# A hybrid decoder layer on one core: z of each pair projected one pair later, and the mixed rows loaded in twos into the low part and split in place

## The reference

```python
h = rms_norm(x, norm_g)
proj = jnp.einsum('bsd,de->bse', h, w_in)
(aq, ak, av, az, bq, bk, bv, bz, bf, cq, ck, cv, cz, cr) = jnp.split(proj, SPLIT_IDX, axis=-1)
out_a = dilated_mixture(rms_norm(aq) * scale, rms_norm(ak), av)        # 12 heads of 64, three dilated windows
out_b = forgetting_attention(rms_norm(bq) * scale, rms_norm(bk), bv, log_f)   # 8 heads of 64
out_c = rms_norm(gla_chunked(cq, ck, cv, log_a), gla_out_gain)         # 4 heads of 192
mixed = concatenate([out_a * silu(az), out_b * silu(bz), out_c * silu(cz)])   # widths 768, 512, 768
return x + einsum('bse,ed->bsd', mixed, w_out)
```

## Time and profile before

| what | value |
|---|---|
| median of 3 runs | 2240.43 us (2240.12 to 2241.71) |
| profiled execution, its own time | 2238.91 us |
| its span | 2237.2 us |
| mean granted clock of TensorE | 0.984 |
| busy: PE, DVE, ACT, POOL | 2155.4, 987.0, 865.1, 238.8 us |
| moved by DMA | 203.23 MB, mean 91 GB/s |

### The profile page before, as it was taken

One profiled execution on the slowest core, in us unless ns is written; L12 is line 12 of the kernel. 1 busy time (PEld: TensorE's weight loads), 2 busy tenths in 40 slices (PEclk: granted clock), 3 DMA queues, 4 the chain that ended last, 5 costly groups with the idle time before them and its releaser, 6 DMA issues.

```text
span 2237.2 us, 30415 instructions
## 1 busy us (share of the span) xinstructions
PE 2155.4 (96%) x11016; PEld 1822.3 (81%) x11016; DVE 987.0 (44%) x1639; ACT 865.1 (39%) x1466; POOL 238.8 (11%) x141
## 2 busy tenths in 40 slices
PE   6999999999989999999999999999999968999999
PEld 5788888888878888888888888888888857778887
DVE  6611346354444544445454545445454555522122
ACT  7311234434354444444444445444444444311110
POOL 0000143331411000101000000001010000000000
PEclk9999999999999999999999999999999979999999
DMA  6322324233322222212222222313222254332234
GB/s 215 82 67 75 94 71 110 62 91 100 84 89 67 71 85 67 85 52 80 70 71 70 66 81 81 95 56 94 70 93 65 67 178 151 118 122 91 80 124 144
DMA packets 190458, 203.23 MB, mean 91 GB/s; under 512 B 16168, under 2 KB 139096, under 8 KB 189232
## 3 DMA queue, kind: packets, MB, share of 16 engines
q1 hardware_dynamic: 173664, 171.80, 26.4%
q10 hardware_dynamic: 16720, 30.45, 3.6%
HBM read 152.38 MB, written 49.83 MB: 90 GB/s over the span
## 4 chain that ended last, share of the span: by engine, by line
PE 85%; DVE 4%; issue 3%; ACT 3%; DMA 3%; POOL 1%; ACTq 0%; DVEq 0%; SPq 0%; POOLq 0%
PE acc L1619 18%; PE acc L1621 17%; PE acc L1620 17%; PE turned L1813 3%; PE pv L1826 3%; PE pv L1825 3%; PE scores L1802 2%; PE scores L1799 2%; DMA w_raw<-in_w_out_dram 2%; PE pv L1707 1%; PE acc L1905 1%; PE acc L1907 1%; PE acc L1906 1%; PE scores L1906 1%; PE scores L1905 1%
## 5 line engine op out<-in xcount | busy, mean ns | idle before, releaser
L1619 PE MATMUL acc<-act_hi,w_hi 128*128 128x512 f32 x1856 | 741.7, 400 | 7.0 <-DVE w_lo L1172 2.5
L1621 PE MATMUL acc<-act_hi,w_lo 128*128 128x512 f32 x1856 | 727.4, 392 | 0.0
L1620 PE MATMUL acc<-act_lo,w_hi 128*128 128x512 f32 x1856 | 726.6, 391 | 0.0
L1172 DVE TENSOR_TENSOR w_lo<-w_raw,w_hi 128x512 fp32r<-128x512 f32 x224 | 181.5, 811 | 581.3 <-ACT w_hi L779 581.0
L1619 PEld LDWEIGHTS acc<-act_hi,w_hi 128*128 128x128 f32 x1856 | 351.1, 189 | 78.3 <-DVE w_lo L1172 5.1
L1621 PEld LDWEIGHTS acc<-act_hi,w_lo 128*128 128x128 f32 x1856 | 350.3, 189 | 76.4
L1620 PEld LDWEIGHTS acc<-act_lo,w_hi 128*128 128x128 f32 x1856 | 351.5, 189 | 67.1
L779 ACT ACTIVATE w_hi<-w_raw 128x512 fp32r<-128x512 f32 x224 | 140.6, 628 | 302.7 <-PE acc L1621 256.4
L1056 ACT ACTIVATE prob<-prob,neg_max 128x128 f32<-128x128 f32 (+7 forms) x160 | 124.4, 777 | 293.3 <-DVE neg_max L1445 293.3
L1461 DVE TENSOR_TENSOR pt_lo<-turned,pt_hi 128x128 fp32r<-128x128 f32 (+7 forms) x160 | 120.9, 755 | 160.1 <-ACT pt_hi L1064 159.3
L1826 PE MATMUL pv<-pt_lo,v_st 128*128 128x128 f32 x720 | 170.5, 276 | 0.0
(11 more groups left out here) (266 smaller groups left out, 2807.9 us busy)
## 6 DMA issues: line engine op xcount, KB each, us to landing
w_raw<-in_w_in_dram SPq DMA_DIRECT2D x240, 256.0 KB, 2.9
proj_scratch<-stage ACTq DMA_DIRECT2D x116, 256.0 KB, 2.1
w_raw<-in_w_out_dram SPq DMA_DIRECT2D x94, 256.0 KB, 3.1
raw<-proj_scratch SPq DMA_DIRECT2D x20, 512.0 KB, 3.4
raw<-mixed_scratch SPq DMA_DIRECT2D x16, 512.0 KB, 4.3
res<-in_x_dram SPq DMA_DIRECT2D x24, 256.0 KB, 5.8
out_dram<-res SPq DMA_DIRECT2D x24, 256.0 KB, 3.0
sq<-proj_scratch SPq DMA_DIRECT2D x10, 512.0 KB, 3.5
```

The lines of the kernel that those rows point to most:

```text
L1172: dve.tensor_tensor(w_lo[:, slot, :], w_raw[:, slot, :], w_hi[:, slot, :].bitcast(F32), ALU.subtract)\
L1619: pe.matmul(acc, hi, xh, start=first, stop=False)
L1620: pe.matmul(acc, hi, xl, start=False, stop=False)
L1621: mm = pe.matmul(acc, lo, xh, start=False, stop=end)
```

## The change

- Counts: `C_FIRST` is gone, the plain stage has one group less. The heads' spare groups are shifted: z of GLA is projected inside the heads, v of pair 0 alone in the group ahead of the pairs (`S_FIRST_V`).
- Body p projects q, k, v of pair p+1 and z of pair p (`columns_of`). z of pair p is loaded into `vz` in body p+1 and bounded, put through the gate and multiplied there; the outputs of pair p wait in the new tile `o_full` (1024 wide) and meet the gate in one product at slot 8 of body p+1 (`gated`).
- The last pair gets the group `S_LAST_Z` in its slots 0 to 7. The early quarters start at slot 8 and end at slot 32, evenly. z of pair 9 is loaded, bounded and put through in slots 15 to 18, in the tile `last_gate`.
- Mixed rows are loaded in twos (1 MB) into `act_lo`, up to four loads at a time, as the last group sets free the tiles; they are split there in slots 4 to 13. Rows 8 and 9 are taken from `vz` in SBUF and are not stored or loaded.
- On DVE the sums of a round come ahead of the next weight split.
- Squares of q and k: the rounded square `sq_hi` lies in the space of `vz`, with a wait for the store of `vz`; values of pair 0 are at slots 3 and 4.

```diff
-C_FIRST = 2 * C_K // P + 2
-C_ALONE = C_FIRST + 1
+C_ALONE = 2 * C_K // P + 2
...
-S_FIRST_Z = C_ALONE + HEAD_GROUPS * C_HEADS
-S_LOOP_A = S_FIRST_Z + 1
+S_FIRST_V = C_ALONE + HEAD_GROUPS * C_HEADS
+S_LOOP_A = S_FIRST_V + 1
 S_PAIRS = S_LOOP_A - PAIR_GROUPS
 S_B0 = S_LOOP_A + PAIR_GROUPS * (A_PAIRS - 1)
 S_LOOP_B = S_B0 + PAIR_GROUPS
-GROUPS = S_LOOP_B + PAIR_GROUPS * (B_PAIRS - 1)
+S_LAST_Z = S_LOOP_B + PAIR_GROUPS * (B_PAIRS - 1)
+GROUPS = S_LAST_Z + 1
+PAIRS = A_PAIRS + B_PAIRS
+LAST = PAIRS - 1
...
+VALUES_OF_FIRST = (3, 4)
+LAST_BOUND, LAST_GATE, LAST_SILU = 15, 16, 18
...
-EARLY_SLOT = [6 + (n * 4) // 5 if n < KT - 1 else 18 + (n - KT + 1) // 2 for n in range(EARLY)]
-MIX_SLOT = [5 + (kk * 4) // 5 for kk in range(KT - 1)]
-
-OUT_ORDER = [k for k in range(KT) if k != A_PAIRS + B_PAIRS - 1] + [A_PAIRS + B_PAIRS - 1]
-
-
-def steps_of(slot):
-
-    out = [("values", b) for b in range(2) if SLOT_VALUES[b] == slot]
+EARLY_SLOT = [8 + (n * 5) // 9 for n in range(EARLY)]
+MIX_SLOT = [4, 4, 5, 6, 6, 7, 8, 9, 9, 10, 10, 11, 12, 12, 13]
+
+OUT_ORDER = list(range(LAST - 1)) + [LAST + 1, LAST + 2, LAST - 1] + list(range(LAST + 3, KT)) + [LAST]
+KK_GATED = OUT_ORDER.index(LAST - 1)
+MIX_LOADS = [k for k in range(0, KT, 2) if k != LAST - 1]
+MIX_BUFS = 4
...
+def columns_of(base, stride, row, z_base, z_stride, z_row):
+
+    return [base + g * stride + row for g in range(3)] + [z_base + 3 * z_stride + z_row]
...
+            def load_gate(pair, row):
+
+                saved(S_LAST_Z if last_pair(pair) else S_LOOP_A + PAIR_GROUPS * pair + 3)
+                load_rows(vz[:], row, P, z_in)
...
+                if not (isinstance(pair, int) and pair < 2):
+                    sp.wait_ge(mixed_saved, 16 * (pair - 1))
...
-                sp.wait_ge(o_done, 4 * (pair + 1))
+                sp.wait_ge(o_done, pair + 1)
                 sp.dma_start(mixed[bass.ds(pair * P, P), :], vz[:]).then_inc(mixed_saved, 16)
 
-            def pair_loads(pair, base, stride, row, next_group, next_base, next_stride, next_row):
+            def pair_loads(pair, group, columns, fox, next_base, next_stride, gate_row):
 
                 def weights(g, kqs):
-                    if next_group is not None:
-                        for kq in kqs:
-                            load_quarter(next_group + g, kq, next_base + g * next_stride + next_row)
-
-                first = isinstance(pair, int) and pair == 0
+                    for kq in kqs:
+                        load_quarter(group + g, kq, columns[g])
+
+                first = first_pair(pair)
                 weights(0, range(2 if first else 0, 3))
+                if fox:
+
+                    sp.wait_ge(masked, ITEMS * pair)
+                    load_bias(pair, 1)
+                if first:
+                    load_values(0, 0, A_WIDTH, 0)
+                else:
+                    load_gate(pair - 1, gate_row)
+                weights(0, (3,))
+                weights(1, range(3))
                 if not first:
                     store_pair(pair - 1)
-                    sp.reg_add(stores_counted, stores_counted, 16)
-                saved_of(pair, 3)
-                if not first:
-
-                    sp.wait_ge(mixed_saved, stores_counted)
-                load_rows(vz[:], base + 3 * stride + row, P, z_in)
-                if base == COL_B:
-
-                    load_bias(pair, 1)
-                weights(0, (3,))
-                weights(1, range(3))
-                if next_group is not None:
-                    load_q(pair + 1, next_base, next_row)
+                load_q(pair + 1, next_base[0], next_base[1])
                 weights(1, (3,))
                 weights(2, range(3))
-                if next_group is not None:
-                    load_k(pair + 1, next_base, next_stride, next_row)
+                load_k(pair + 1, next_base[0], next_stride, next_base[1])
                 weights(2, (3,))
                 weights(3, range(4))
-                if next_group is not None:
-                    load_values(pair + 1, next_base, next_stride, next_row)
+                load_values(pair + 1, next_base[0], next_stride, next_base[1])
...
+            def load_mixed(i):
+
+                k = MIX_LOADS[i]
+                if i >= MIX_BUFS:
+                    sp.wait_ge(mix_hi, 2 * (i - MIX_BUFS) + 2)
+                if k < 12:
+                    sp.wait_ge(quarter_done, 3 * (S_LAST_Z + AHEAD) + k // 4 + 1)
+                else:
+                    sp.wait_ge(half_done, 2 * GROUPS)
+                sp.dma_start(act_lo[:, k:k + 2, :].bitcast(F32), mixed[k * P:(k + 2) * P, :].rearrange("(k p) t -> p k t", p=P))\
+                    .then_inc(mix_in[i % MIX_BUFS], 16)
...
+            last_column = COL_B + 3 * B_WIDTH + (B_PAIRS - 1) * P
+            for kq in range(3):
+                load_quarter(S_LAST_Z, kq, last_column)
+            load_gate(LAST - 1, last_column - P)
+            sp.wait_ge(masked, ITEMS * LAST)
+            load_bias(LAST, 1)
+            load_quarter(S_LAST_Z, 3, last_column)
             sp.wait_ge(gla_saved, 16 * C_HEADS)
+            sp.wait_ge(mixed_saved, 16 * (LAST - 1))
             load_mixed(0)
             load_mixed(1)
+            load_out_rows(0, 0, 0)
+            load_mixed(2)
+            load_mixed(3)
+            load_out_rows(1, 1, 0)
+            load_mixed(4)
+            load_mixed(5)
+            load_mixed(6)
             for n in range(2, EARLY):
                 load_out_rows(n, n % (KT - 1), 0)
...
+                if n == 6:
+                    sp.wait_ge(mix_lo, KK_GATED + 1)
+                    load_gate(LAST, last_column)
+                if n == 7:
+
+                    sp.wait_ge(silu_done, LAST)
...
+            def gated(pair, rows, cols, halves):
+
+                dve.wait_ge(silu_done, pair + 1)
+                dve.wait_ge(o_summed, 4 * pair + halves)
+                dve.tensor_tensor(vz[rows, cols], o_full[rows, cols], vz[rows, cols], ALU.mult).then_inc(o_done, 1)
...
+                    dve.tensor_tensor(o_full[own, cols], pv[own, :], o_full[own, cols], ALU.add).then_inc(o_summed, 1)
+                    if last_pair(pair) and h == 1:
+                        gated(pair, own, cols, u + 1)
...
+            def last_body():
+                def steps(slot):
+                    steps_at(LAST, slot, False)
+                    for kk in range(KT - 1):
+                        if MIX_SLOT[kk] == slot:
+                            mix_hi_part(kk)
+
+                group(S_LAST_Z, COL_B + 3 * B_WIDTH + (B_PAIRS - 1) * P, steps)
...
             def split_next(n):
-                split_lo_out(n + 1)
                 if n % (KT - 1) == 0 and n > 0:
                     early_sums(n // (KT - 1) - 1)
+                split_lo_out(n + 1)
...
-                dve.tensor_tensor(act_lo[:, OUT_ORDER[kk], :], raw[:, kk % 2, :],
-                                      act_hi[:, OUT_ORDER[kk], :].bitcast(F32), ALU.subtract).then_inc(mix_lo, 1)
+                k = OUT_ORDER[kk]
+                dve.tensor_tensor(act_lo[:, k, :], mix_row(k), act_hi[:, k, :].bitcast(F32), ALU.subtract)\
+                    .then_inc(mix_lo, 1)
...
-            store_pair(A_PAIRS + B_PAIRS - 1)
-            sp.wait_ge(mixed_saved, 16 * (A_PAIRS + B_PAIRS))
-            load_mixed(KT - 1)
```

258 lines of the change are left out of this document (135 added, 123 removed).

## The result

The changed kernel takes 2214.3 us in the median of four runs (2212.9 to 2218.7) beside 2240.3 of the kernel before, a ratio of 0.989 with a 95% interval of 0.988 to 0.990. The profiled execution of it takes 2212.9 us (span 2211.1) against 2238.9 (span 2237.2): 26.0 us are gone where 34.3 were forecast.

The account below looks back on a forecast made before the run. PE was taken as the bound, losing time where it idles or its clock drops; -21.8 - 1.1 - 11.4 = -34.3 us from 2238.9 gives 2204.6, plus 1.5 for the median: 2206 us, range 2195 to 2224 (forecast's own 2199 to 2213).

Parts of the forecast that it names:

- The group taken from the front and pair 0: One group less ahead of the first GLA head, -21.8 us; pair 0's values taken at slots 3 and 4, -1.1.
- Pairs 1 to 8: Loop pairs with z projected for the same pair and one gated product: cost 0, as DVE has idle margin.
- Rival C: Each loop pair gains a wait, SP standing at the store until DVE's gated product: +63 us, 2269; chance 0.02.
- The last pair: From first turned values to first output quarter: 139.5 us work, 15.3 idle, 3.6 more, 158.4 instead of 169.8.
- Hole ahead of the third quarter: Last pair: PE idles 4.2 us because the third early quarter's weights queue on SP behind two mixed loads.
- DVE in slots 8 to 13: Last pair: 31 us of DVE steps against about 33 of PE work; 3 us idle, bounds 0 and 12.5.
- Turn into round three: Last pair: with sums ahead of the next weight split, PE's wait of 3.85 us becomes about 0.4.
- Late weights in rounds two and three: Last pair: gaps of 0.8 us or so from late weights stay, 3.6 us over both rounds.
- Clock: Last pair: 3.6 us added to work and idle time; 19.2 us charged to the lower clock before the change.
- B: DVE and ACT bound the last pair: 12.5 us idle, 10 by the clock, 174 us long; 2222 in all; chance 0.16.
- A: Nothing stalls: third quarter's weights in time, DVE keeps up, last pair 148.5 us, 2196 in all; chance 0.16.
- D: Last pair: a two-row load takes 8.6 us, rows arrive no sooner, weight loads queue behind; 2234; chance 0.04.

Follow-up runs that it names:

- e5: Changed kernel with an unused 64x512 DVE product put behind the last o_full add of each pair but the last; 2219.8 us, ratio 0.991.
- e6: Changed kernel with an unused 64x512 DVE product put behind the first o_full add of each pair but the last; 2214.5 us, ratio 0.988.
- e2: Changed kernel with the third early weight load issued ahead of the last two 1 MB mixed loads; 2211.4 us, ratio 0.988.
- e8: e3 with ACT copying a slot's mixed rows ahead of its attention steps in the last pair; 2204.7 us, ratio 0.984.
- e1: Changed kernel with SP's wait for row 8's split, last gate load and four residual loads three early weight loads later; 2206.6 us, ratio 0.985.
- e9: Changed kernel with only SP's wait for row 8's split and the last gate load three early weight loads later; 2205.7 us, ratio 0.986.
- e4: Changed kernel with the split of the next weights ahead of the early sums again; 2214.7 us, ratio 0.989.
- e10: e8 with the fourth early weight load also issued ahead of the last mixed load; 2202.5 us, ratio 0.985.
- e12: e10 with the residual loads of rounds two and three issued three early weight loads later; 2200.4 us, ratio 0.982.
- e7: Changed kernel with each 1 MB mixed load issued as two of 512 KB in the same place; 2213.4 us, ratio 0.989.
- e3: Changed kernel with both load-queue moves, those of e1 and e2; 2205.6 us, ratio 0.985.

## Why the prediction came out as it did

The forecast was 2206 us and the time is 2214.3: inside the range of 2195 to 2224 and faster as said, but outside the forecast's own 2199 to 2213. Two of its steps were wrong, in opposite directions: pairs 1 to 8 were put at nothing and gave 7.3 us, and the last pair was taken 16.0 us too short, above all because the wait and the load of the last gate on SP's queue were left out.

- **The group taken from the front and pair 0**, -22.9 us forecast, -22.2 measured (21.3 ahead of pair 0, 0.9 in it): right.
- **Pairs 1 to 8**, costed at 0, gave -7.3. The step that failed is the sentence that puts them at 0 because DVE is busy for 60.8 of 125.8 us. DVE is idle half of a pair, but not at its turn: there the old product stood in the chain of sum, product, weight split and `v_st` split, for which PE waits. The order of DVE at the turn was to be read in the timeline, not the share. e5 gave 4.4 of it back, e6 nothing; 2.9 stay open. Rival C looked at the same place for a loss, and there is none: every pair became shorter.
- **The last pair**, 158.4 us forecast, 174.4 measured: 16.0 too good. Its idle time is 25.0 where 15.3 was summed up (+9.7), and its working time 149.4 where 143.1 was (+6.3). By term:
  - z group: 1.5 forecast, 0.9 measured (its one gap).
  - Hole ahead of the third quarter: 4.2 forecast, 2.22 measured (2.52 in e6, 3.90 in e5). The cause was right (e2). That the gap is smaller is not because the weights came sooner. The z group ends at 1790.7 us and ACT can copy the weights at 1801.99, 11.3 us later, where the sum had them in after 8.5 to 10; the quarter begins 12.7 us after the group's end, where it had 10.5. But PE took 10.4 us until then and not 6.4, through its stop of 2.54 and slow matmuls, so it waited less.

```profile
1801.99 1.25 ACT L863 ACTIVATE w_hi<-w_raw 128x512 fp32r<-128x512 f32 x2 [1.96 <-DMA w_raw<-in_w_out_dram]
```

  - The weights landed 0.7 us behind the second of the two loads and did not pass it, which agrees with the ring order that the Trainium skill ("DMA: Bandwidth & Descriptors", queues, rings and completion order) states. The size of the gap does not follow from it.
  - DVE in slots 8 to 13: 3 forecast. The gaps ahead of 1794.06 and 1818.47 are 4.4, and 2.3 more stands ahead of 1841.93. e8 shows that ACT's order makes about half of these. The room that the sum saw was not there either: it put PE's work in slots 8 to 13 at about 33 us, but its own numbers give 22.4 for the quarters and 6.8 for six slots of attention, 29, less than the 31 of DVE.
  - Not in the sum: the 3.59 us stop. The prediction followed the weights past the mixed loads, and not past the gate load and its wait for row 8's split, which the diff puts on the same queue four loads later. By e1 and e9 that omission alone costs 6.3 to 7.0 us of the last pair, and by the ratios 6.5 to 8 of the time. It is the largest error.
  - Turn into round three: 0.4 forecast, 0.77 measured, 3.85 before. Right; but e4 shows that undoing the line brings stops of 3.7 us and yet nothing measurable of the time.
  - Late weights in rounds two and three: 3.6 forecast; the gaps from 1850 to the last but one, without the turn, make 8.4, above all the 2.13 and 1.29 us behind the turn.
  - The end: 2.6 forecast, 2.49 measured.
  - Clock: the 3.6 that the sum adds to work and idle time. No run shows that term. Matmuls of 512 columns at the lower rate cost 5.6, and from 1.5 (e10) to 7.2 (e6) in the other traces. The other 4 us or so of the working time were missing from my 139.5: without the slow matmuls the last pair's working time is 143.8 in the changed kernel and 142.9 in e12. The prediction had charged 19.2 us of the last pair before to the clock; counting one by one finds 12.0 in its matmuls of 512 columns. The rest holds the shorter matmuls and, as the 143 us show, some 3.5 to 4 of plain work. The 22 us, an estimate by the rule of the Trainium skill ("TensorE: Matmul & The Clock Gate", the part on the HAM clock gate), err further to the same side.
- **Rows 8 and 9 from SBUF**, 0 forecast. No run tests this by itself; at the end of the pair no loss shows. But row 8 from `vz` is what put SP's wait into the queue.
- **Behind the last pair** nothing was forecast; -1.1 us measured. Before, seven slow matmuls followed the last gap; in the changed kernel none. That is not the change's doing: in e1 to e12, whose programs are the same there, it is from 0 to 13.

The errors sum to 0.7 - 7.3 + 16.0 - 1.1 = 8.3 us, the distance between the forecast for the profiled execution, 2204.6, and its 2212.9. That it is no more is luck: the gain that was missed in the loop paid for half of the last pair.

Of the rivals, B gave the length of the last pair almost exactly (174 us), yet by another mechanism: it wanted 22.5 us lost in slots 8 to 19 to DVE and ACT, 12.5 of them idle. The idle time there is near that (12), but e1 shortened the pair by 6.3 us by moving one wait on SP. The 3.1 us of stops that e8 took out by an order on ACT belong to B. A (148.5 for the last pair) was not reached by any version; the best has 161.3. D fell: a mixed load took 5.1 us in the median and not 8.6 (7.1, 7.2 and 7.9 where it stood behind another), and no row was late. The 3.5 us that the prediction took for each megabyte in a row were too much: of two loads issued one behind the other the second landed 2.6 us after the first.

## What to carry to other kernels

When an in-order queue feeds the bottleneck, list every entry ahead of each load that counts, with the semaphore that it waits on and when that fires; a cheap load behind a late wait holds up all loads behind it, and here one such line cost 6.5 to 8 us beside a gain of 26. An engine at half load can still set the pace where a chain passes through it: look at its order at the turn of the loop, and put work that nobody waits for behind the step that somebody does. The length of a gap depends on when the engine got there as well as on what it waits for, so compare the moment at which the work behind it starts, counted from a fixed event. And look at several traces of the same stretch before a difference of a few microseconds is given to an edit: here one stretch of the same program took 174.4 us in one and 177.5 in another.

## What the runs showed of the hardware

- On SP's queue in the last pair the first load of 512 KB landed in 3.5 us (e7) and the first of 1 MB in 5.0 (changed kernel). The four loads of 1 MB with no other of them right ahead took 4.9 to 5.1 us, the two issued 0.4 us behind another 7.1 and 7.2, and these landed 2.6 us after the first. Two loads of 512 KB in a row were in after 5.0 us, as one of 1 MB.
- The length of one stop does not say by itself whether the clock falls. Of stops of about 2.3 us ahead of the same quarter, the one of the changed kernel (1841.93 us) was followed by seven slow matmuls, the one that ended it counted, the one of e3 (1831.32 us, 2.31) by eight, the first 1.3 us after it, and the one of e9 (1836.06 us, 2.30) by none. The 3.59 and 4.06 us stops (e4) were followed by seven each. Where the longest one was taken out there were fewer in all: 27 became 12 in e1.
